# Order changes in four stages of a two-block kernel: gate quarters in the stick-breaking attention, the low parts at the end of the second feed-forward product, the head sums and one turn beside the long convolution

## The reference, cut to what matters

```python
def stick_breaking_attention(q, k, v):      # 8 heads of 64; 4 blocks of 128 queries
    z = einsum(qb, kb) * scale               # query t, key s < t
    log_not = where(strict, log_sigmoid(-z), 0)
    suffix = cumsum(log_not, reverse=True) - log_not
    a = where(strict, exp(log_sigmoid(z) + suffix), 0)
    return einsum(a, vb)

def first_block(x, ...):
    proj = rms_norm(x, g_mix_pre) @ w_in     # q, k, v, pool, gating, 3 gates x 1024
    gates = sigmoid(gate_in)
    merged = gates[0]*(o_sb @ w_br_sb) + gates[1]*(o_pool @ w_br_pool) + gates[2]*(o_gm @ w_br_gm)
    x = x + rms_norm(merged @ w_out, g_mix_post)
    h = rms_norm(x, g_ff_pre)
    return x + rms_norm(square(relu(h @ w_ff_in)) @ w_ff_out, g_ff_post)

def second_block(x, ctx, ...):
    hx = modulate(rmsnorm(x), ...);  hc = modulate(rmsnorm(ctx), ...)
    attn = rmsnorm(diff_attn(q_x, k_all, v_all, lam), subln)
    u = short_conv(hy_x); v, x1, x2 = split(u)            # Hyena
    for n, gate in enumerate((x1, x2)):
        z = gate * (irfft(rfft(z) * k_f[n]) + skip[n] * z)
    x = x + g_a * (concat(attn, rmsnorm(z)) @ w_out)
    return rmsnorm(x + g_f * conv_ffn(modulate(rmsnorm(x), ...)))
```

## Time and profile before

| | us |
|---|---|
| median of 3 runs (1556.2 to 1558.71) | 1556.92 |
| the profiled execution | 1556.86 |
| its span on the core | 1555.1 |
| PE busy | 1483.3 (95%) |
| DVE busy | 859.7 (55%) |
| ACT busy | 620.4 (40%) |
| POOL busy | 313.7 (20%) |

### The profile page before, as it was taken

The page is one execution under the profiler, slowest core; times in us unless marked ns, Lnnn a source line. Parts: engine busy times, 40 slices in busy tenths (PEclk is TensorE's granted clock), DMA queues, the critical chain, the costliest instruction groups (busy, mean ns, idle before and its releaser), DMA issues.

```text
span 1555.1 us, 18009 instructions
## 1 busy us (share of the span) xinstructions
PE 1483.3 (95%) x7022; PEld 1207.9 (78%) x7022; DVE 859.7 (55%) x1396; ACT 620.4 (40%) x986; POOL 313.7 (20%) x298
## 2 busy tenths in 40 slices
PE   6998999999999999999997999988898999999998
PEld 4776678888778878888875878876687888888886
DVE  5455666554567564664456437756756545335534
ACT  5545763222544221343353326543444333123332
POOL 0262221101122100121014312115621011111101
PEclk9999999999999999999998999989999999999999
DMA  7351115545155354454327211224432232322221
GB/s 256 109 173 57 42 40 194 200 156 176 61 187 165 124 172 161 154 170 156 120 83 224 65 67 42 82 66 138 145 140 83 94 108 89 101 95 95 98 93 54
DMA packets 53327, 187.93 MB, mean 121 GB/s; under 512 B 5943, under 2 KB 6616, under 8 KB 53114
## 3 DMA queue, kind: packets, MB, share of 16 engines
q1 hardware_dynamic: 47450, 165.80, 32.1%
q0 software_dynamic: 4736, 16.78, 3.3%
q10 hardware_dynamic: 1056, 4.19, 0.8%
HBM read 174.16 MB, written 12.58 MB: 120 GB/s over the span
## 4 chain that ended last, share of the span: by engine, by line
PE 88%; DVE 5%; ACT 3%; issue 1%; POOL 1%; DMA 0%; SPq 0%; ACTq 0%; DVEq 0%; POOLq 0%
PE PS L455 87%; PE PS L466 2%; DVE wl L1679 1%; ACT wh L1102 1%; DVE TMP L2172 0%; DMA X<-in_x 0%; DVE TMP L1732 0%; DVE Y L1888 0%; POOL wl L2312 0%; POOL HCl L2439 0%; DVE accm L1659 0%; ACT TMP L1196 0%; ACT TMP L1194 0%; ACT TMP L1388 0%; DVE Y L1694 0%
## 5 line engine op out<-in xcount | busy, mean ns | idle before, releaser
L455 PE MATMUL PS<-HTh,wh 128*128 128x512 f32 x1056 | 419.8, 398 | 12.8 <-DVE wl L1679 8.2
L1679 DVE TENSOR_TENSOR wl<-raw,wh 128x1024 fp32r<-128x1024 f32 x210 | 272.0, 1299 | 284.5 <-ACT wh L1102 284.2
L455 PE MATMUL PS<-HTl,wh 128*128 128x512 f32 x1056 | 413.4, 392 | 0.0
L455 PE MATMUL PS<-HTh,wl 128*128 128x512 f32 x1056 | 413.3, 391 | 0.0
L1102 ACT ACTIVATE wh<-raw 128x1024 fp32r<-128x1024 f32 x228 | 239.2, 1053 | 291.6 <-PE PS L455 256.5
L455 PEld LDWEIGHTS PS<-HTh,wh 128*128 128x128 f32 x1056 | 200.0, 189 | 60.5 <-issue 16.7
L455 PEld LDWEIGHTS PS<-HTh,wl 128*128 128x128 f32 x1056 | 199.5, 189 | 42.8
L455 PEld LDWEIGHTS PS<-HTl,wh 128*128 128x128 f32 x1056 | 199.9, 189 | 39.1 <-issue 0.5
L455 PE MATMUL PS<-wh,FFh 128*128 128x512 f32 x432 | 169.9, 393 | 0.0
L455 PE MATMUL PS<-wh,FFl 128*128 128x512 f32 x432 | 168.9, 391 | 0.0
L455 PE MATMUL PS<-wl,FFh 128*128 128x512 f32 x432 | 168.6, 390 | 0.0
(11 more groups left out here) (322 smaller groups left out, 2133.6 us busy)
## 6 DMA issues: line engine op xcount, KB each, us to landing
raw<-in_ws SPq DMA_DIRECT2D x268, 512.0 KB, 3.8
taps<-TMP SPq DMA_DIRECT2D x16, 256.0 KB, 2.4
tab<-in_spec POOLq DMA_DIRECT2D x8, 512.0 KB, 5.5
raw<-taps SPq DMA_DIRECT2D x8, 512.0 KB, 3.8
kd<-TMP POOLq DMA_DIRECT2D x16, 256.0 KB, 5.1
wh<-in_wd POOLq DMA_DIRECT2D x8, 512.0 KB, 4.0
wl<-in_wd POOLq DMA_DIRECT2D x8, 512.0 KB, 4.7
kf<-kd SPq DMA_DIRECT2D x8, 512.0 KB, 3.8
```

What stands on the lines that cost most here:

```text
L455: return nc.tensor.matmul(out, l, r, start=start, stop=stop, skip_group_check=True)
L1679: tt(WL[k][:, :n], RAW[RAW_AT["unit", u, 0] % RAWS][:, :n], f32(WH[k][:, :n]), ALU.subtract).then_inc(sem("lo_dve"), 1)
```

## The change

Four things are moved; no instruction is added or taken away.

1. Stick-breaking attention: two quarters of the gates stand ahead of the scores of pair 1 on PE, ahead of scores 2 and 3 on ACT and DVE. Of the other 22, the pairs of the first three pairs of heads have 1, 1, 2, 2 (with 128, 256, 384, 512 queries), the last four pairs one each.
2. The unit of (1,0,2) leaves `POOL_LOW`, so DVE makes its low part; POOL makes each piece of `HCl` ahead of the spectrum unit that it followed.
3. `sub_sums` stands behind `forward(0, 0)`.
4. In order 1, `hyena_turn(10)` stands beside block 2 instead of 3, and DVE's `hyena_conv(10)` beside block 0 instead of 1.

```diff
@@ POOL_LOW @@
-    or any(u == AT[(o, e, k), 0, 0][0][0] for o in range(2) for e, k in ((0, 2), (1, 0), (1, 2))))]
+    or any(u == AT[(o, e, k), 0, 0][0][0] for o, e, k in ((0, 0, 2), (0, 1, 0), (0, 1, 2), (1, 1, 0), (1, 1, 2))))]
@@ program @@
+        EARLY_FIRST = range(2)
+        EARLY_FROM = [2 + sum((1, 1, 2, 2)[q % 4] if q < 12 else 1 for q in range(p)) for p in range(PAIRS + 1)]
+
         def EARLY_AT(p):
 
-            return range((3 * p + 1) // 2, (3 * p + 4) // 2)
+            return range(EARLY_FROM[p], EARLY_FROM[p + 1])
@@ tensor_program @@
                 first(k)
                 second(k)
+            for f in EARLY_FIRST:
+                early(f)
             scores(1)
...
             hyena_turn(7)
-            sub_sums()
...
                     forward(o, f)
+                    if f == 0 and o == 0:
+                        sub_sums()
                     if f == 1 - o:
                         sub_scale(3 * o)
                     if f == 3 and o == 0:
                         sub_scale(1)
-                    if f and o and f != 2:
-                        hyena_turn(9 + f // 2)
+                    if f in (1, 2) and o:
+                        hyena_turn(8 + f)
                     if f >= 2:
                         backward(o, f - 2)
@@ vector_program @@
-                    if f == 1 and o:
+                    if f == 0 and o:
                         hyena_conv(10)
@@ gpsimd_program @@
-            weights(unit((1, 0, 2), 0, 0))
             e.wait_ge("p_fo", 16)
             for i in range(0, 8, 4):
-                weights(unit((1, 1, i // 2), 0, 0))
                 e.wait_ge("nc_hi", i // 4 + 1)
                 tt(HCl[:, i:i + 4, :], ZC[:, i:i + 4, :], f32(HCh[:, i:i + 4, :]), ALU.subtract).then_inc(sem("nc_lp"), 1)
+                weights(unit((1, 1, i // 2), 0, 0))
```

## The result

The changed kernel took 1540.29 us (median of 4 runs, 1539.02 to 1541.3) beside 1557.82 for the kernel before (4 runs), a ratio of 0.9890 [0.9876, 0.9903]. A second set gave 1540.48 (5 runs, 1538.14 to 1542.98), ratio 0.9887 [0.9872, 0.9902]. The forecast was 1541.1.

A forecast was written before the change was run, and what follows sets the result against it. PE, busy 95% of the span, was taken to bound the kernel, leaving only its waits and low-clock stretches to win. Terms -0.7 - 3.5 - 11.6 + 0 = -15.8 from 1556.86 gave 1541.1 us, range 1537.5 to 1548.5.

The forecast's parts named there:

- Attention, -0.7: Stick-breaking attention: early gate quarters fill PE's wait for V, scores 2 start 1.26 earlier; -0.7 us, bounds 0 and -1.3.
- Low parts, -3.5: Ahead of w_in_2: POOL's earlier HCl shortens PE's 8.23 us wait; -3.5 us, bounds -4.5 and -2.0.
- the 2.8 of the forecast: POOL's chain ahead of w_in_2: tile 1 of HTl starts at 820.7 instead of 823.5, -2.8 us.
- the 0.7 put down for them: At w_in_2: 0.7 us for half-clock matmuls behind the wait, which may go or stay once the gap is some 3 us.
- The new wait: First spectrum half: PE waits 4.2 us, from 807.44 to 811.7, for the low part DVE now makes.
- DVE loses nothing: DVE makes the (1,0,2) low part in 1.22 us, inside its idle 1.45 ahead of the reciprocal, at no cost.
- Rival B: Ahead of w_in_2: PE, not POOL, is late at a low clock; low parts become +3, total 1547.6 us; chance 8%.
- Sums, -11.6: Start of Hyena: block 0 fills the wait ahead of the head sums, first backward block starts earlier; -11.6 us.
- Rival A: Start of Hyena: clock low throughout, so the sums' move gains only 7.8, total 1544.9 us; chance 25%.
- Order 1, 0: Order 1: earlier turn and convolution gain 0.65, but one 3.3 us gap may lower the clock; 0, bounds -0.65 and +1.2.
- Rival D: Order 0: low clock does not come back between forward and backward blocks; slower, 1564.1 us; chance 4%.
- rival C: Further on: a wait hidden in the earlier trace takes back part of the gain; 1545 to 1555 us; chance 8%.

The follow-up runs named there:

- e1: Kernel before with only the attention's reordering (two early gate quarters ahead of scores 1): 1554.55 us, ratio 0.9982.
- e9: Changed kernel without the attention's reordering: 1542.87 us, ratio 0.9905 to the kernel before.
- e2: Kernel before with only the low parts' order changed (HCl ahead of the spectrum units, unit of (1,0,2) to DVE): 1553.39 us, ratio 0.9975.
- e6: Kernel before with POOL making each HCl ahead of its spectrum unit, but the unit of (1,0,2) left on POOL: 1557.58 us, ratio 0.9999.
- e5: Changed kernel without the order 1 move (turn and convolution of row 10 put back): 1540.74 us, ratio 0.9892 to the kernel before.
- e10: Kernel before with only the head sums moved behind forward block 0, timed a second time: 1547.72 us, ratio 0.9934.
- e11: Changed kernel with four more 512-column matmuls at the start of the w_out product's second half: 1542.44 us, ratio 0.99 to the kernel before.
- e7: Changed kernel with the head sums behind forward block 1 instead of 0: 1542.59 us, ratio 0.9901 to the kernel before.
- e4: Kernel before with only the turn and convolution of row 10 one block earlier in order 1: 1557.88 us, ratio 1.0004.
- e8: Changed kernel with POOL's first HCl split into two halves: 1541.15 us, ratio 0.9893 to the kernel before.

## Why the prediction was right, and where it wasn't

**The sum.** Forecast -15.8; the trace shows -15.6 and the medians -17.1 and -17.5, inside the range. That the trace comes within 0.2 is partly luck: the four terms as measured there (-0.49, -4.0, -10.9, +0.87) add up to -14.5. The 1.7 behind 432, which no term holds, stand against +0.6 of drift in stages that weren't changed. The traces of single runs differ by some 2 us from the medians: that of before is 0.8 below its median of 29 runs.

**Attention, -0.7.** Right: -0.49, -0.99 in the two traces of the changed kernel, -0.83 in e1. These are taken against one trace of before; the mean distance from scores 1 to the gap is 291.49 in the seven traces with the old attention and 290.42 in the six with the new one and no delay, so -1.1. Scores 2 came 1.35 earlier for 1.26, scores 3 only 0.85 for 1.2 to 1.3. What I hadn't seen is that the filled wait needn't keep the clock up: 0.69 between 142 and 148 here, and down to 150 still low (scores 2 take 0.69 instead of 0.44). It did keep it up in three of seven traces, where scores 3 came 1.37 earlier (151.31 - 141.40 = 9.91 us behind scores 1 in the changed kernel's second trace, 11.28 in before); with the empty wait it fell in all seven (0.50 to 0.72).

**The 1.7 us behind 432.** Missing from the sum. I took the clock behind gaps that the change doesn't touch to be the same as before. The step that failed is that one. It made e1 2.8 instead of 0.7 to 0.8, and e9's median points the same way (1542.87 - 1540.48 = 2.4, of two sets whose intervals overlap). Whether part 1 does it by shifting the gap isn't shown.

**Low parts, -3.5.** -4.0 by e2 and by the changed kernel (-5.67 + 1.68). w_in_2 starts 832.05 - 826.63 = 5.42 earlier, 3.7 of it from here, for the 2.8 of the forecast. The 2.8 was one HCl in POOL's row. Without the 1.7 and a shift of 0.05, tile 1 of HTl is read 4.3 earlier (817.49 for 823.50): the first wl of the row starts 1.0 sooner behind the gap at 432, and the row up to tile 1 lasts 817.49 - 810.49 = 7.0 us instead of 823.50 - 813.22 = 10.3, since one HCl less stands in it and none of the rest is stretched to 2.85 any more. Of this 0.6 is lost again behind tile 5. In before the row began with this wl:

```profile
813.22 2.37 POOL L2312 TENSOR_TENSOR wl<-raw,wh 128x1024 fp32r<-128x1024 f32 x1 [5.42 <-ACT wh L1102]
```

At w_in_2 the half-clock matmuls behind the wait stayed, and of the 0.7 put down for them 0.3 came. The new wait was 3.57, not 4.2: DVE's tensor_scalar was already held in before, to 2.80, and is now held to 2.21, by HCl, which ends sooner behind its start than the wl did. That "DVE loses nothing" was luck of the place, as e6 shows, where the same idle time of POOL costs DVE 2.2 us. Rival B fell: the clock came back within the 12 matmuls (in e2 it didn't fall), and the transposes ran at 0.12 each, as before. The stretch that holds the last matmuls and nearly all transposes:

```profile
812.00:818.00 6.00, 5.54 (x38) 4.66 (x36) 3.54 (x6) 3.98 (x7) 6.00 (x4) 0.89 0.31 95
```

**Sums, -11.6.** -10.9 here, -10.7 to -12.3 in the seven other traces with them behind block 0. The sums took 4.17 for 3.5, since the clock fell while they ran, and block 1 ran at half clock as taken. It did so in four of the eight traces, with gains of 10.7 to 10.9; in the other four (e5, e9, e10, e11) the clock came back inside block 1, and the gain was 12.0 to 12.3. In e5:

```profile
1034.80:1038.00 3.20, 3.20 (x11) 2.62 (x11) 3.13 (x5) 2.52 (x3) 2.41 (x2) 0.51 0.92 280
1038.00:1041.00 3.00, 1.95 (x8) 1.33 (x7) 2.14 (x8) 1.50 (x5) 0.10 (x1) 0.96 0.21 83
```

As named, DVE was next: the backward block waits 0.63 for `no` here. Rival A fell in all eight. What I set against the forecast, that one-column products keep the clock low, held in part: e7 shows that they lower it, but they don't start at the low level.

**Order 1, 0.** The trace shows +0.87 and e4's median +0.2, inside the bounds. The price I named, a fall of the clock in the single gap, came in all seven traces; what I had not weighed is that the two gaps it replaces can do the same. Rival D fell: between the blocks of order 0 the clock stayed at 1.00, and rival C too: no wait behind 1062 is longer than before but the one of part 4.

## What to carry to other kernels

Put work that is ready into a wait, and ask what the next engine's chain starts from: block 0 in front of the sums won 11 us since DVE's products start 7.2 us behind the last turn instead of 17.5, while the attention's 3.2 us wait, filled, gave some 0.5 to 1.1. An idle stretch of POOL isn't free if DVE has a chain of short instructions there. And what one trace shows behind a gap of 2 to 3 us of PE is one draw: compare the same stretch in several traces before a microsecond or two is put down to a change.

## What the runs showed of the hardware

- Two DVE instructions from SBUF to SBUF were held by the POOL tensor_tensor beside them: one of a single column took 2.35 us instead of 0.16 and ended with it, one of 128x1024 took 2.79 instead of 0.75 and ended 0.54 behind it (e6). The Trainium skill ("SBUF — State Buffer", SBUF: two separate sides) has the rule: DVE and GpSimd share a pair of ports that one of them holds for a whole instruction. The rows agree, and they show the reverse too (POOL's second half, 1.72 instead of 1.29); e8 shows how little it helps to split POOL's work: the wait moves to DVE's next instruction.
- One-column float32 matmuls, 32 records without a gap, started at a granted clock of 1.00 in nine traces, and it fell to 0.50 in each while they ran or right at their end, though PE is busy; they take some 3.6 to 4.4 us so, and 6.99 when they start at 0.50.
- The same gap of 2.3 us lowered the clock or didn't, in 9 and 5 of 14 traces; the same filled wait of the attention did in 4 and didn't in 3 of 7.
